# Fetching the first expert block two tiles ahead, with one-hot products for the last tiles' tokens

## The reference

```
h = rmsnorm(x);  p = h @ w_in                    # q, k, v, o, gates, u
hm, C, n, m = mlstm_run(q, k, v, gates, state)   # 4 heads of 128, chunk after chunk
hp, buf = pool_mix(u, ...)                       # trailing means over 2, 4, 8, 16 rows
x = x + concat(hm, hp) @ w_out
h2 = rmsnorm(x)                                  # * norm2_g
y[t] = sum over 2 of 16 experts of gate[t, e] * (silu(h2 @ w_gate[e]) * (h2 @ w_up[e])) @ w_down[e]
x = x + y;  y_prompt, y_sample = rmsnorm(x) * norm_f_g
```

## Time and profile before

| what | value |
|---|---|
| three runs | 954.97, 955.98, 956.29 us; median 955.98 |
| profiled execution | 955.15 us, its span 953.5 us, mean clock of TensorE 0.966 |
| PE busy in the span | 881.4 us (92%) |
| DVE, ACT, POOL busy | 435.6, 145.7, 370.2 us |
| DMA | 163.27 MB, 171 GB/s over the span |
| 0 to 60 us | weights of the mixer are loaded |
| 60 to 530 us | mixer, PE busy nearly throughout |
| 530 to 548 us | from the last tile to the first expert |
| 548 to 907 us | experts; between 600 and 700 us PE is busy 100.0 us, POOL 78.8 us, DMA share 1.02 |
| 907 to 953 us | last block, final norm, outputs |

### The profile page before, as it was taken

How to read it: one execution, slowest core, us unless ns; L and a number is a source line. 1 busy time by engine, 2 the same in 40 slices (tenths; PEclk the granted TensorE clock), 3 DMA queues, 4 the chain that set the end, 5 groups by cost and what they waited for, 6 DMA issues and landing times. The chain is left out here.

```text
span 953.5 us, 16776 instructions
## 1 busy us (share of the span) xinstructions
PE 881.4 (92%) x6367; PEld 758.9 (80%) x6367; DVE 435.6 (46%) x1168; ACT 145.7 (15%) x447; POOL 370.2 (39%) x569
## 2 busy tenths in 40 slices
PE   5999999999999999999986799999999999999920
PEld 3975969779596795968853399999999999999920
DVE  2245474737537365463656723334333333333255
ACT  2123122221312212121121000000000000000051
POOL 4050040300303012030220466678887777764512
PEclk9999999999999999999989799999999999999975
DMA  9931101020300202011065169999999999999882
GB/s 334 287 128 20 49 14 32 1 78 2 70 8 12 67 1 56 1 13 44 1 192 173 50 212 312 343 348 359 336 350 343 332 334 329 321 310 301 244 326 114
DMA packets 90713, 163.27 MB, mean 171 GB/s; under 512 B 48834, under 2 KB 59570, under 8 KB 82463
## 3 DMA queue, kind: packets, MB, share of 16 engines
q1 hardware_dynamic: 72047, 138.25, 41.4%
q0 software_dynamic: 17568, 24.23, 11.1%
q10 hardware_dynamic: 1040, 0.00, 0.1%
HBM read 139.39 MB, written 25.44 MB: 173 GB/s over the span
## 5 line engine op out<-in xcount | busy, mean ns | idle before, releaser
L1428 PE MATMUL bank<-wout,win 128*128 128x130 f32 (+3 forms) x2048 | 246.4, 282 | 3.2 <-DVE wout L1316 3.2
L1428 PEld LDWEIGHTS bank<-wout,win 128*128 128x128 f32 x2048 | 244.8, 191 | 3.2 <-DVE wout L1316 3.2
L1428 PE MATMUL bank<-hT,win 128*128 128x128 f32 (+1 forms) x1536 | 182.9, 279 | 0.0
L1428 PEld LDWEIGHTS bank<-hT,win 128*128 128x128 f32 x1536 | 178.6, 192 | 1.5 <-issue 1.2
L582 POOL DMA_INDIRECT z_d<-wout,win x75 | 119.2, 1589 | 27.9 <-issue 26.6
L1428 PE MATMUL bank<-win 128*128 128x130 f32 (+3 forms) x1024 | 123.7, 281 | 0.0
L1428 PE MATMUL bank<-win,hT 128*128 128x260 f32 (+3 forms) x512 | 119.9, 412 | 3.2 <-DMA win<-in_w_in 1.7
L1428 PEld LDWEIGHTS bank<-win 128*128 128x128 f32 x1024 | 122.3, 190 | 0.0
L1428 PE MATMUL bank<-wout,mixT 128*128 128x512 f32 (+1 forms) x384 | 116.8, 487 | 1.8 <-ACT mixT L819 1.7
L1428 PEld LDWEIGHTS bank<-win,hT 128*128 128x128 f32 (+1 forms) x512 | 76.1, 171 | 41.8 <-issue 32.7
L1428 PEld LDWEIGHTS bank<-wout,mixT 128*128 128x128 f32 (+1 forms) x384 | 50.8, 163 | 57.1 <-issue 54.4
(11 more groups left out here) (296 smaller groups left out, 813.1 us busy)
## 6 DMA issues: line engine op xcount, KB each, us to landing
win<-in_w_gate SPq DMA_DIRECT2D x32, 1024.0 KB
win<-in_w_up SPq DMA_DIRECT2D x32, 1024.0 KB
win<-in_w_down SPq DMA_DIRECT2D x32, 1024.0 KB
win<-in_w_in SPq DMA_DIRECT2D x4, 2048.0 KB, 19.6
xbuf<-in_x_prompt SPq DMA_DIRECT2D x8, 512.0 KB, 3.9
wout<-in_w_out SPq DMA_DIRECT2D x1, 4096.0 KB, 15.5
z_d<-xbuf SPq DMA_DIRECT2D x32, 128.0 KB
h_d<-xn SPq DMA_DIRECT2D x8, 512.0 KB, 2.8
```

What stands on the lines that cost most here:

```text
L1428: return nc.tensor.matmul(out, lhsT, rhs, start=first, stop=last)
```

## The change

Block one's rows are put together from two sources. In POOL's round i = LAST, after scatter(LAST-2), the ids of block one as far as they are known (tiles 0 to LAST-2) are read and gathered into xg1; slots not yet filled point to the zero row of h2_d. DVE turns these rows in round NT and scales them later in the same round. The tokens of the last two tiles are added by PE: for each tile DVE makes a matrix pick (128 tokens by 150 places, the token's rstd where it holds that place of expert 0, zero elsewhere), ACT makes a copy of x1 with the columns in the turned order, and PE multiplies the copy with pick, eight products of 128 by 150 per tile, summed over both tiles in banks 2, 3 and 0. DVE's first_rows adds the two parts into xgT, in eight operations, ahead of the table. The PE state transposes stand before ranks(LAST) now, their copies out of PSUM and the eight state stores are ACT's, and the 14 matmuls without use are gone. On the zero rows only zeros are stored, 4 bytes at a time. A copy of x_prompt's last 256 rows into h2_d is queued after load_x(3) and counted in ids_zeroed. In block one DVE's products come before the turn of block two. The ids of block one are still loaded a second time, for the gates.

```diff
 # SP
             for rows in (h2_d, z_d):
-                sp.dma_start(rows[TOK, :].rearrange("(p n a) -> p n a", p=P, a=2), empty[:, 0:D // (2 * P), :]
-                             ).then_inc(S["ids_zeroed"], 16)
+                sp.dma_start(rows[TOK, :].rearrange("(p n a) -> p n a", p=P, a=1), empty[:, 0:D // P, 1:2],
+                             allow_slow_non_contiguous=True).then_inc(S["ids_zeroed"], 16)
             load_x(3)
+            early = [START[t] for t in PICKED]
+            sp.dma_start(h2_d[min(early):max(early) + P, :], x_prompt[0, min(early):max(early) + P, :]).then_inc(S["ids_zeroed"], 16)
...
             after(sp, "table_ready", 1)
-            for c in range(NP):
-                sp.wait_ge(first[c], 16)
...
 # POOL
-            after(pool, "ids_zeroed", 16 * 3)
+            after(pool, "ids_zeroed", 16 * 4)
             for i in range(NT + 2):
...
                 if 2 <= i:
                     scatter(i - 2)
+                if i == LAST:
+                    after(pool, "h2_stored", 16 * (LAST - 1))
+                    after(pool, "u_done", NT)
+                    load_ids(0)
+                    pool.wait_ge(ids_in, 16)
+                    add_quarter(False)
+                    pool.wait_ge(carried, 1)
+                    gather_tokens(first, xg1)
...
             load_ids(0)
-            pool.wait_ge(ids_in, 16)
-            add_quarter()
+            pool.wait_ge(ids_in, 32)
+            g.tensor_copy(ents[0], idraw).then_inc(carried, 1)
             pool.wait_ge(carried, 2)
-            gather_tokens(first)
 # ACT, in norm_2
+                if t in PICKED:
+                    a.activation(xp[t - PICKED[0]], xbuf[:, t % 4, :].rearrange("p (f k) -> p k f", k=KD), ACT.Copy
+                                 ).then_inc(xp_ready, 1)
 # DVE
+            def first_picks(t):
+                i, place = t - PICKED[0], rt[:, 80:81]
+                link(v.scalar_tensor_tensor(out=rt[:, 128 + i:129 + i], in0=oh[:, t, 2, 0:1], scalar=-NEAR, in1=place,
+                                            op0=ALU.mult, op1=ALU.add))
+                v.tensor_scalar(pick[i], place_of[:, :, :], rt[:, 128 + i:129 + i], sm[:, 11:12], ALU.is_equal, ALU.mult
+                                ).then_inc(pick_ready, 1)
...
+            def first_rows():
+                dve.wait_ge(base_scaled, 1)
+                after(dve, "out_done", NT)
+                for n, (b, k0, k1) in enumerate(PICKB):
+                    dve.wait_ge(picked, n + 1)
+                    for k in range(k0, k1):
+                        at = B[b][:, (k - k0) * BLOCK:(k - k0 + 1) * BLOCK].rearrange("p (a i) -> p a i", a=NP)
+                        v.scalar_tensor_tensor(out=xgT[:, k, :, 0:RP], in0=at, scalar=g2m[:, k:k + 1], in1=xgS[:, k, :, 0:RP],
+                                               op0=ALU.mult, op1=ALU.add).then_inc(gx_ready, 1)
...
                     h2_evac(LAST - 1)
+                    first_turn()
                     numerators(LAST)
...
                     routing(LAST - 1)
+                    first_scale()
                     residual(LAST)
...
+            first_rows()
             NJ = NB + 1
             dve.wait_ge(S["rank_read"], NT)
...
-            first_turn()
...
+            products(1, SLOTS[0][0])
             gather_turn(1)
-            products(1, SLOTS[0][0])
             gather_scale(1)
 # PE
+            def first_picks(t):
+                i = t - PICKED[0]
+                pe.wait_ge(xp_ready, i + 1)
+                pe.wait_ge(pick_ready, i + 1)
+                for b, k0, k1 in PICKB:
+                    for k in range(k0, k1):
+                        at = B[b][:, (k - k0) * BLOCK:(k - k0 + 1) * BLOCK].rearrange("p (a i) -> p a i", a=NP)
+                        last = mm(at, xp[i][:, k, :], pick[i], i == 0 and k == k0, i == 1 and k == k1 - 1)
+                    if i == 1:
+                        last.then_inc(picked, 1)
...
+                if i == NT + 1:
+                    first_picks(LAST - 1)
+                    state_transposes()
                 if 2 <= i:
                     ranks(i - 2)
+                if i == NT + 1:
+                    first_picks(LAST)
...
-            for _ in range(WARM):
-                mm(B[7][:, 0:512].rearrange("p (a b) -> p a b", a=4), ident[:, :],
-                   ident[:, :].unsqueeze(1).broadcast_to([P, 4, P]))
...
-                pe.wait_ge(gx_ready, NP + j - 1)
+                pe.wait_ge(gx_ready, KD + j - 1)
```

More of the change, by code:

```diff
@@ L212, in hymba_step @@
         assert off + KD * NP * 32 <= 15 * D
+        PICKED = (LAST - 1, LAST)
+        xp = [win[:, (15 + i) * D:(16 + i) * D].rearrange("p (k f) -> p k f", k=KD) for i in range(2)]
+        xg1 = win[:, 17 * D:17 * D + NP * PIECE].rearrange("p (a d) -> p a d", a=NP)
+        pick = [win[:, 19 * D + i * BLOCK:19 * D + (i + 1) * BLOCK].rearrange("p (a i) -> p a i", a=NP) for i in range(2)]
+        PICKB = ((2, 0, 3), (3, 3, 6), (0, 6, 8))
         yb = [win[:, t * D:(t + 1) * D] for t in range(NT)]
@@ L545, in scatter, with gather_tokens, load_ids, add_quarter @@
                     after(pool, name, 16 * (t + 1))
+            h2_q = h2_d.rearrange("t (q d) -> (t q) d", q=NQ)
+            def gather_tokens(to, dst=xg):
+                for c in range(NP):
+                    g.indirect_dma_start(out=dst[:, c, :], out_offset=None, in_=h2_q,
+                                         in_offset=bass.IndirectOffsetOnAxis(ap=idt[:, c:c + 1].bitcast(U32), axis=0)
+                                         ).then_inc(to[c], 16)
+            def load_ids(row):
+                src = ids_d[bass.ds(row, 32 * NP), :].rearrange("(i a) n -> i (a n)", a=NP)
+                pool.dma_start(idraw.rearrange("p a n -> p (a n)"), src.unsqueeze(0).broadcast_to([NQ, 32, 2 * NP])
+                               ).then_inc(ids_in, 16)
+            def add_quarter(keep=True):
+                g.tensor_scalar(idt, idraw[:, :, 0], qf[:, 0:1], None, ALU.add).then_inc(carried, 1)
+                if keep:
+                    g.tensor_copy(ents[0], idraw).then_inc(carried, 1)
             after(pool, "hist_ready", 1)
-            after(pool, "ids_zeroed", 16 * 3)
+            after(pool, "ids_zeroed", 16 * 4)
             for i in range(NT + 2):
@@ L555, in _ @@
                     scatter(i - 2)
[L558 to L564, removed]
-            def load_ids(row):
-                src = ids_d[bass.ds(row, 32 * NP), :].rearrange("(i a) n -> i (a n)", a=NP)
-                pool.dma_start(idraw.rearrange("p a n -> p (a n)"), src.unsqueeze(0).broadcast_to([NQ, 32, 2 * NP])
-                               ).then_inc(ids_in, 16)
-            def add_quarter():
-                g.tensor_scalar(idt, idraw[:, :, 0], qf[:, 0:1], None, ALU.add).then_inc(carried, 1)
-                g.tensor_copy(ents[0], idraw).then_inc(carried, 1)
+                if i == LAST:
[6 more added lines that the diff above has]
+                    gather_tokens(first, xg1)
             def stand(c):
@@ L1046, in places @@
                 v.tensor_tensor(cnt[:, :], B[7][:, NE:2 * NE], cnt[:, :], ALU.add).then_inc(S["rank_read"], 1)
+                if t in PICKED:
+                    first_picks(t)
                 for n in range(2):
@@ L1177, in _ @@
             link(v.tensor_scalar(ecap[:, :], iof[:, 0:NE], float(CAP), None, ALU.mult))
+            for a in range(NP):
+                v.tensor_scalar(place_of[:, a, :], iof[:, 0:RP], float(NP), a - NEAR, ALU.mult, ALU.add)
             p0 = 0
@@ L1248, in _ @@
                     norm_x1(i - 1)
-            after(dve, "ulT_done", 1)
-            for n in range(2):
-                last = v.tensor_copy(uout[:, n, :], B[4 + n][0:HIST, :])
-            last.then_inc(S["ul_out"], 1)
-            after(dve, "nT_done", 1)
-            v.tensor_copy(gt[:, :, :], B[6][0:H, 0:2 * P].rearrange("p (a b) -> p a b", a=2)).then_inc(S["nT_out"], 1)
+            first_rows()
             NJ = NB + 1
```

78 lines of the change are left out of this document (47 added, 31 removed).

## The result

The changed kernel takes 982.19 us (median of 4 runs, 981.79 to 982.99) against 955.48 us (954.47 to 956.29): a ratio of 1.0286, 95% interval 1.0272 to 1.0300. I had forecast 958.0 in a range of 951 to 964. The sign is that of the forecast, the size is not: 26.7 us instead of some 2.

What follows compares the result with a forecast made beforehand. PE was taken as busy nearly throughout, bound at the mixer-to-experts hole by a relay of waits; the start-up wait counted too. +7.5 (start-up) - 5.5 (transition) = +2.0 us on 955.15: 957.1, or 958.0 on the median; range 951 to 964.

Steps and rivals of the forecast that it cites:

- The start-up: Program start: POOL's first pooling waits for added DMAs and PE works longer at half clock; +7.5 us (4.2 to 10.8).
- the transition: Mixer to experts: expert one starts 13.0 us earlier, but only 5.5 us (3 to 12.7) is left at expert two.
- The small pieces: Start-up: stores of two zero rows in 1024 pieces of 4 bytes each take 1.4 us (0 to twice that).
- The copy: Start-up: copy of 256 x_prompt rows into h2_d, which POOL's first pooling waits for, takes 4.0 us (2.5 to 5.3).
- nothing covers a delay of POOL here: Start-up: PE takes up POOL's first result at once, so POOL's delay, 6.3 us (3.4 to 8.6), is not hidden.
- The early gathers: End of mixer: last gather of block one lands after 6.0 us, delaying DVE's numerators by 0.9 us (0.4 to 2.5).
- Picks, state transposes, products: From DVE's read of the last counts (527.42) through picks and matmuls to the last of eight products at 532.6.
- Block two's rows are late next: After the table, ids and gathers run beside weights; expert two starts at 567.0 (561.3 to 569.5), PE idles 7.7 us.
- PE is the busier of the two, so POOL can catch up, nothing more is lost: Experts after expert two: PE busy 100 of 100 us between 600 and 700, POOL 79; no further loss.
- Rival 4: Transition: picks and state transposes push ranks and products to about 540, gain gone; +7.5, 963.5 us; chance 0.05.
- Rivals 1 and 2: Start-up wait cheap, POOL under 3 us late: 953.0, chance 0.18; block two on time: 950.8, chance 0.15.
- rival 3: Slower by both: copy at z_d's rate, block one's gathers hold DVE 2.5 us; +10 - 4, 962.0 us; chance 0.17.

Runs made afterwards that it cites:

- s1: Changed kernel with the zero rows of both scratch tables written in 128 pieces of 32 bytes each instead of 1024 of 4 bytes; 964.01 us.
- s4: Kernel before with the 4-byte pieces alone, 2048 in place of 256 of 32 bytes; 970.89 us.
- s3: Changed kernel with 32-byte pieces as before and the copy of x_prompt rows on a semaphore of its own; 964.66 us.
- s2: Changed kernel, 4-byte pieces kept, the copy of x_prompt rows on its own semaphore, awaited by POOL only ahead of the early gathers; 976.25 us.
- s13: Kernel before with 45 tiny linked operations on POOL, once, ahead of block one's scatters; 957.18 us.
- s12: Kernel before with 20 tiny linked operations on POOL, once, ahead of block one's scatters; 955.22 us.
- s6: Changed kernel with zero row from a zero tile, copy on its own semaphore, and DVE's first-block transposes moved behind the last tile's numerators; 955.18 us.
- s8: s6 with expert two's weight loads also held on SP until POOL is about to issue block two's gathers; 952.44 us.
- s14: s8 with 20 tiny linked operations on POOL, once, ahead of block one's scatters; 957.40 us.
- s11: s8 with expert two's weights held until block two's rows have landed, not just until their gathers are about to be issued; 949.33 us.
- s9: Kernel before with 4-byte pieces in z_d's zero row alone; 961.75 us.
- s10: Kernel before with both zero rows in pieces of 8 bytes, 1024 in all; 961.38 us.

## Why the prediction was wrong, point by point

The start-up was to cost 7.5 us and cost some 23; the transition was to give back 5.5 and gave nothing, and the experts lost 3 more. The first error is the larger: with dense rows and nothing else mended (s1) the loss is 9.3 us instead of 26.7.

- **The small pieces: the step that failed.** The term was "two rows 1.4 us (bounds 0 and twice that)", from 128-byte pieces, 1024 of which take 0.7 us. The 4-byte pieces took 15.2 us at POOL and 16.2 in the total (s4). Two things were wrong in it. The rate of a piece was carried over to pieces 32 times smaller, 1024 to a row of 4 KB, and the upper bound was twice that same rate, so it could not catch the error. And I had only the engines' time in the sum, not SP's queue, which stood for 9.54 us and made x tile 3 late as well.
- **The copy.** 4.0 us, bounds 2.5 to 5.3: it holds POOL for 3.5 us by itself (s1 against s3). Behind the pieces it holds it for 7.7 us (s2), outside the bounds, and costs 5.2 us of time. The upper bound of POOL's delay was added up wrong as well: 5.3 and 2.8 give 9.0 us, not 8.6; neither is near 22.4.
- **That nothing covers a delay of POOL here** was right: 22.4 us at POOL, 22.2 at PE, 23.0 at the last scatters. That they agree to a microsecond is in part luck, since with no delay at all that scatter starts anywhere from 480.86 (s13) to 482.91 (s12), and 15.2 us at POOL are 16.9 at the scatter in s4.
- **The early gathers.** This is the second step that failed. I had the last of them landed 6.0 us after its issue, and 0.9 us of delay to the numerators with 2.5 as the upper bound. The first weights were issued between the gathers, the last gather landed 8.9 us after its issue, and the numerators were 4.35 us late. The half clock that followed was not in the sum at all: PE went over to it in the wait of 5.56 us and did out_of_heads(LAST) at it, so at the ranks of the last tile 6.9 us were lost (557.27 - 22.98 against 527.42), not 2.1. s6 gives both back. The picks and state transposes ahead of those ranks, 0.8 us in the sum, cost nothing: PE waits for DVE's one-hot choices there, not DVE for PE.
- **Picks, state transposes, products.** From that row to expert one I had 5.2 us; it took 4.7. Expert one ran warm (granted clock 1.00 from its start), in 24.8 us, where I had 24.6. No run has the warming matmuls put back.
- **Block two's rows are late next** was the right mechanism. From the table to expert two I had 22.6 us and it was 25.9: the ids took 6.2 instead of 3.2 (with the 1.0 that I had added for the weights), the register reads 2.7 instead of 1.7 (my 1.7 ended at 542.63, which is the last gather of block one; the load of the ids is issued at 543.59), the last gather 6.8 instead of 7.5. With the table 4.1 us later than forecast, expert two started 7.4 us later than forecast, which is more than the whole gain of 5.5, and the half clock behind it cost 2.4 us instead of 1.5.
- **"PE is the busier of the two, so POOL can catch up, nothing more is lost"** was wrong as a rule, though only 0.7 us of it shows in the changed kernel itself (rest, 293.4 against 292.7). A chain that is made of landings and waits as well as of busy time has the slack that its place against PE gives it, and the mean share doesn't show it: POOL is busy for 78.8 of the 100 us from 600 to 700 in the kernel before, where 6 us more cost nothing (s12), and for 75.3 in s8, where they cost 3.7 to 5.0 (s14).
- **The rivals.** Rival 4 comes nearest on the transition: its gain is gone. But it had ranks held by picks at half clock, and they were held by numerators. Rivals 1 and 2 are out; rival 3, slower by both, had the direction, but it put no more on the pieces than I did. That the sign came out as forecast is no merit of the sum, in which two terms of like size were set against each other.

## What to carry over

A store whose elements lie apart was priced by its pieces here, not by its bytes, and whoever waits for that store or for one behind it in the queue pays: 8 KB of zeros cost 16 us, and a zero tile of 32 bytes per partition brings POOL's start back to 55.84. When a step is moved earlier, look at what its data wait for in the new place: a transpose that waits for a gather must not stand ahead of work that doesn't. And before counting on an earlier start, ask which chain paces the part that follows; if its rounds are as long as those of the engine that gains, order the transfers so that this chain starts earlier too, as s11 does by holding six megabytes of weights for the sake of 0.65.

## What was unexpected of the hardware

- 5.9 to 8.5 ns per piece of 4 or 8 bytes, where 128-byte pieces of the same trace take 0.7 ns. Why these are about ten times dearer is not settled: small size, alignment, that they share one row, and that they ran behind the load of w_out were not tried apart.
- SP's queue stands at the DMA that comes next after a store of 1024 such pieces, whatever that is: 9.54 us at the second store in the changed kernel (9.81 in s4), and 9.09 us at the load of x tile 3 in s9, whose one thin store itself took 0.76. Behind 512 pieces of 8 bytes it is 5.29 us (s10). Behind the second thin store the load takes 3.90, about the 3.45 of before. The row of s9:

```profile
41.55 9.09 SPq L316 DMA_DIRECT2D xbuf<-in_x_prompt  x1
```

- While the pieces are written PE pauses in the middle of a run of matmuls: 3.46 us "issue" ahead of 61.42. POOL's wait lasts much longer (to 78.03), so the pause is hidden behind it; what PE was waiting for the trace doesn't show.
- The last of five gathers of 128 quarter rows was turned 2.8 us after its issue with no weights in flight (s11), 6.8 beside them (changed kernel, block two), and 9.0 where the first weight loads were issued between the gathers (changed kernel, block one).
